# Softmax probabilities scaled on ScalarE instead of VectorE in a two-block transformer kernel

## The chip, the core and the metric

One core of a Trainium2 chip (trn2) runs the whole program in one launch. The metric is the device time of a launch in microseconds. The kernel before takes 810.37 us (median of three runs, 810.2 to 810.66).

## What is computed

256 tokens of width 1024 go through two transformer blocks. The first block is attention with 16 softmax heads of 64 columns and a feed-forward part with a short convolution. The second block is a feed-forward part, a mixer with 8 "stick-breaking" heads and 8 "forgetting" heads, and another feed-forward part. The change touches the 24 heads that end in a softmax: the 16 of the first block and the 8 forgetting ones. For these the reference computes:

```
p = softmax(where(k_pos <= q_pos, z, -inf), axis=-1)      # z = q k^T (+ forgetting terms)
out = einsum('bhqk,bhkd->bhqd', p, v)
```

The softmax divides each row of exponentials by the row's sum. With 256 queries and causal masking a head's exponentials take 128 x 384 numbers: 128 x 256 for the later 128 queries (all 256 keys) and 128 x 128 for the earlier ones.

## The kernel before, in words

The order of every instruction is fixed by one list of steps that a planner class writes before the program is built (`Plan.lay`). Each engine walks the same list and emits its own part of each step; an engine runs its instructions strictly in that order, and semaphores hold it where it needs another engine's result.

The bulk of the work is weight matmuls. A weight slab (8 tiles of 128 rows by 256 columns) is loaded by DMA into `raw`; ScalarE writes a rounded copy `whi` (L769) and VectorE the remainder `wlo` = raw - whi (L1015), both in pieces of two tiles (128 x 512); TensorE then does three matmuls per tile and half (hi x hi, hi x lo, lo x hi; L1442, L1445 and L1446, or L1431 to L1433 where the value columns are made). Twelve such matmuls make a chunk. After each chunk the planner puts one more `hi` step (and the `lo` step of the piece before it) and then lets the attention heads advance by one turn (`attend`), so attention is woven into the weight matmuls.

Heads go in pairs (n, n+1). Counted in turns from the pair's start (its age), the planner puts:

- age 0, `scores`: TensorE computes both heads' scores (L1496, for forgetting heads also L1504); VectorE adds the mask and takes the negated row maxima (L1333 and L1335, the two parts of a head, result in `rs`); ScalarE does the exponentials and row sums (L959 and L960).
- age 2, `scale` of head n: VectorE takes the reciprocals of the row sums (L1342) and multiplies the two parts of `W` by them (L1344: 128 x 256; L1345: 128 x 128), then raises `s_scale`.
- age 3, `turn` of head n, then `scale` of head n+1, then possibly `scores` of the next pair: TensorE transposes W in three pieces (L1513), which waits for `s_scale`; ScalarE copies the result out of PSUM (L967).
- age 4, `turn` of head n+1.
- age 6, `values`: TensorE multiplies by the values (L1550), ScalarE and VectorE split the result (L978 `Ohi`, L1365 `Olo`).

A second pair enters when the first has age 3, and the next two only when all is through, so the 24 softmax heads come in six sets of two pairs, four sets in the first block (about 22 us apart, from 26 us on) and two in the second (from 542 and from 593 us on). Each set has four turns of L1513; I call them turn 1 to turn 4 of the set.

Of the kernel before, what the change touches and what calls it, by code (L numbers as in the profile page):

```python
# [7 lines left out]
ALU = mybir.AluOpType  # L8
ACT = mybir.ActivationFunctionType
# [5 lines left out]
P = 128  # L15
S = 256
# [435 lines left out]
def build_program(nc, a, out):  # L452
    with ExitStack() as ctx:
        def sb(name, shape, dt=F32):
            return ctx.enter_context(nc.sbuf_tensor(name, shape, dt))

        def sem(name):
            return ctx.enter_context(nc.semaphore(name))
# [45 lines left out]
        rs = sb("rs", [P, 4, 4])  # L504
# [12 lines left out]
        W8 = sb("W8", [P, 8, 3 * P])  # L517
# [27 lines left out]
        s_scores, s_max, s_exp, s_inv, s_scale = (sem(n) for n in ("s_scores", "s_max", "s_exp", "s_inv", "s_scale"))  # L545
# [9 lines left out]
        soft = {n: k + 1 for k, n in enumerate(m for m, h in enumerate(heads) if h[0] != "sb")}  # L555
# [184 lines left out]
        def _(act):  # L740
            need = Once(act)
# [195 lines left out]
            def first_pass(n):  # L937
# [21 lines left out]
                act.activation(p[:, 0:S], b[:, 0:S], ACT.Exp, bias=m[:, 0:1], scale=-1.0, accum_out=s[:, 0:1])  # L959
                act.activation(p[:, S:3 * P], b[:, S:3 * P], ACT.Exp, bias=m[:, 1:2], scale=-1.0, accum_out=s[:, 1:2]).then_inc(s_exp, 1)  # L960

            def turned(n):
                i = n % 4
                need.wait_ge(s_tpe, t_use["turn", n] + 1)
                if n >= 4:
                    need.wait_ge(s_val, n // 2 - 1)
                act.activation(W8[:, 2 * i + 1, :], banks[T_BANK][:, 0:3 * P], ACT.Copy).then_inc(s_w, 1)  # L967
# [18 lines left out]
            def qk_norm(base):  # L986
# [8 lines left out]
                act.activation(lb, lb, ACT.Exp, scale=-0.5).then_inc(s_qr, 1)  # L995

            part_of = {"hi": weights, "ain": a_in, "gq": norm_columns, "sq": squares, "norm": norm, "latey": late_hi, "modul": shift_hi,
                       "ccol": condition, "evict": evict, "fpart": forget, "scores": first_passes, "turn": turned, "later": later,
                       "values": values, "vturn": v_turned, "qkn": qk_norm}
            for step in st.list:  # L1000
                if step[0] in part_of:
# [3 lines left out]
        def _(dve):  # L1005
            need = Once(dve)
# [268 lines left out]
            def values_out(g):  # L1275

                ph, _, c0 = groups[g]
                c = (qkv_base(ph, c0) - 16) * P
                if ph == "qkv1" and c == 0:
                    root_columns()  # L1280
                for i in range(2):
                    o = Vn[:, i, c:c + C]
                    if ph == "qkv1":
                        need.wait_ge(s_rcol, 2)
                        ins = dve.tensor_scalar(o, at(g, i), rcol[:, i:i + 1], None, ALU.mult)
                    else:
                        ins = dve.tensor_copy(o, at(g, i))
                ins.then_inc(s_evicted, 1)
# [47 lines left out]
                                         op0=ALU.add, op1=ALU.min, accum_out=m[:, 1:2]).then_inc(s_max, 1)  # L1336

            def scale(n):
                i = n % 4
                s, p = rs[:, i, 2:4], W8[:, 2 * i, :]  # L1340
                need.wait_ge(s_exp, soft[n])
                dve.reciprocal(s, s).then_inc(s_inv, 1)  # L1342
                need.wait_ge(s_inv, soft[n])
                dve.tensor_scalar(p[:, 0:S], p[:, 0:S], s[:, 0:1], None, ALU.mult)  # L1344
                dve.tensor_scalar(p[:, S:3 * P], p[:, S:3 * P], s[:, 1:2], None, ALU.mult).then_inc(s_scale, 1)  # L1345

            def stick_sum(n):
                i, k = n % 4, stick[n]
# [18 lines left out]
            def qk_norm(base):  # L1367
                need.wait_ge(s_qr, nth("qkn", base))
                need.wait_ge(s_gq, 1)
                for n in (base, base + 1):  # L1370
# [6 lines left out]
            part_of = {"lo": weights, "ain": a_in, "add": add_squares, "latey": late_y, "latelo": late_lo, "modul": modulate,  # L1377
                       "hcol": gates, "gq": first_columns, "mod": mod_dot, "modout": mod_out, "xscale": scale_x, "evict": evict, "fpart": forget,
                       "scores": peaks, "scale": scale, "stsum": stick_sum, "later": later, "values": values, "qkn": qk_norm}
            for step in st.list:  # L1380
                if step[0] in part_of:
# [231 lines left out]
```

## Time and profile before

| | us |
|---|---|
| median of three runs | 810.37 |
| the profiled execution, its own time | 810.29 |
| its span, from first to last instruction | 808.1 |
| TensorE matmul busy | 795.0 (98%) |
| VectorE busy | 649.5 (80%) |
| ScalarE busy | 483.2 (60%) |

The first row of the table is what is predicted. The profile is one execution; between its span and its own time lie 2.2 us. Matmuls overlap one another in the pipe, so "busy" of TensorE is the time in which at least one was under way. The granted TensorE clock is 1.00 in all but the last stretch. In the views, PE is TensorE's matmul side, PEld its weight loads, DVE is VectorE, ACT is ScalarE.

### The profile page before, as it was taken

How to read it: one execution, taken by the hardware profiler on the slowest of the kernel's cores; microseconds unless marked ns; L12 is line 12 of the kernel's file. 1: busy time of each engine (PE TensorE's matmuls, PEld its weight loads, DVE VectorE, ACT ScalarE, POOL GpSimd, SP SyncE). 2: the span in 40 equal slices, each digit the busy share in tenths (PEclk: the TensorE clock that was granted, in tenths of full speed). 3: DMA queues.
4: the chain of work that ended last, by engine and by line, in shares of the span. 5: the costliest groups of instructions: out<-in, count | busy, mean ns of one | idle time of the engine just before them, and what ended most of it. 6: DMA issues, size and time to landing. Idle time of an engine off the chain costs nothing.

```text
span 808.1 us, 16849 instructions
## 1 busy us (share of the span) xinstructions
PE 795.0 (98%) x6800; PEld 773.9 (96%) x6800; DVE 649.5 (80%) x1395; ACT 483.2 (60%) x1008; POOL 21.4 (3%) x53
## 2 busy tenths in 40 slices
PE   7999999999999999999999999899999999999998
PEld 7999999999999999999999999889789999999998
DVE  5899887988889897999988887977667996775551
ACT  6755566677666666745554646665656775555440
POOL 1000000000000000000000000700000000000000
PEclk9999999999999999999999999999999999999999
DMA  9777784656666987599999887545334578655540
GB/s 293 263 249 233 221 286 137 207 188 201 208 205 202 323 280 269 166 330 342 346 316 314 281 260 238 161 131 178 117 108 152 184 260 263 211 184 193 196 157 27
DMA packets 150014, 179.44 MB, mean 222 GB/s; under 512 B 5681, under 2 KB 139569, under 8 KB 149937
## 3 DMA queue, kind: packets, MB, share of 16 engines
q1 hardware_dynamic: 147680, 177.22, 66.7%
q8 instruction: 54, 0.88, 0.5%
q10 hardware_dynamic: 1232, 1.11, 0.4%
q0 software_dynamic: 1024, 0.03, 0.1%
q14 instruction: 24, 0.19, 0.1%
HBM read 177.27 MB, written 1.05 MB: 221 GB/s over the span
## 4 chain that ended last, share of the span: by engine, by line
PE 89%; DVE 5%; ACT 3%; DMA 1%; issue 1%; SPq 0%; DVEq 0%; ACTq 0%
PE bank L1442 26%; PE bank L1445 26%; PE bank L1446 26%; DVE wlo L1015 2%; PE bank L1431 2%; PE bank L1550 1%; PE bank L1433 1%; PE bank L1432 1%; DMA raw<-in_moba_w_qkv 1%; PE bank L1496 1%; PE bank L1513 1%; ACT whi L769 1%; PE bank L1534 1%; ACT W L959 0%; ACT W L960 0%
## 5 line engine op out<-in xcount | busy, mean ns | idle before, releaser
L1015 DVE TENSOR_TENSOR wlo<-raw,whi 128x512 fp32r<-128x512 f32 x528 | 342.3, 683 | 66.1 <-ACT whi L769 65.3
L769 ACT ACTIVATE whi<-raw 128x512 fp32r<-128x512 f32 x528 | 306.5, 622 | 95.8 <-PE bank L1446 86.5
L1442 PE MATMUL bank<-A,whi 128*128 128x256 f32 x1152 | 323.0, 280 | 3.4 <-DVE wlo L1015 2.4
L1445 PE MATMUL bank<-A,whi 128*128 128x256 f32 x1152 | 318.9, 277 | 0.1
L1446 PE MATMUL bank<-A,wlo 128*128 128x256 f32 x1152 | 318.5, 276 | 0.0
L1442 PEld LDWEIGHTS bank<-A,whi 128*128 128x128 f32 x1152 | 216.5, 188 | 5.6 <-DVE wlo L1015 3.0
L1445 PEld LDWEIGHTS bank<-A,whi 128*128 128x128 f32 x1152 | 216.4, 188 | 0.7 <-issue 0.5
L1446 PEld LDWEIGHTS bank<-A,wlo 128*128 128x128 f32 x1152 | 216.3, 188 | 0.0
L1442 PE MATMUL bank<-Hhi,whi 128*128 128x256 f32 x528 | 146.0, 276 | 0.0
L1446 PE MATMUL bank<-Hhi,wlo 128*128 128x256 f32 x528 | 145.7, 276 | 0.0
L1445 PE MATMUL bank<-Hlo,whi 128*128 128x256 f32 x528 | 145.7, 276 | 0.0
L1445 PEld LDWEIGHTS bank<-Hlo,whi 128*128 128x128 f32 x528 | 99.1, 188 | 0.0
L1442 PEld LDWEIGHTS bank<-Hhi,whi 128*128 128x128 f32 x528 | 99.1, 188 | 0.0
L1446 PEld LDWEIGHTS bank<-Hhi,wlo 128*128 128x128 f32 x528 | 99.1, 188 | 0.0
L1114 DVE SCALAR_TENSOR_TENSOR mring<-mring,cact 128x1024 f32<-128x1024 f32 x72 | 87.1, 1218 | 0.0
L1442 PE MATMUL bank<-B,whi 128*128 128x258 f32 (+1 forms) x184 | 52.8, 287 | 0.1
L926 ACT ACTIVATE Hhi<-hb 128x256 fp32r<-128x256 f32 x33 | 13.8, 418 | 64.3 <-DVE hb L1209 38.7
L1445 PE MATMUL bank<-B,whi 128*128 128x258 f32 (+1 forms) x184 | 52.3, 284 | 0.0
L1446 PE MATMUL bank<-B,wlo 128*128 128x258 f32 (+1 forms) x184 | 51.8, 282 | 0.0
L1175 DVE SCALAR_TENSOR_TENSOR ca<-bank,cols,ca 128x255 f32<-128x255 f32 (+1 forms) x88 | 36.4, 473 | 2.0 <-ACT ca L892 2.0
L1442 PE MATMUL bank<-Ohi,whi 128*128 128x256 f32 x128 | 36.8, 287 | 0.0
L1445 PE MATMUL bank<-Olo,whi 128*128 128x256 f32 x128 | 35.7, 279 | 0.0
(170 smaller groups left out, 960.8 us busy)
## 6 DMA issues: line engine op xcount, KB each, us to landing
mring<-in_w_mod SPq DMA_DIRECT2D x72, 512.0 KB, 6.1
raw<-in_ffn_w_up SPq DMA_DIRECT2D x22, 1024.0 KB, 5.1
raw<-in_w_gate SPq DMA_DIRECT2D x22, 1024.0 KB, 5.6
raw<-in_w_up SPq DMA_DIRECT2D x22, 1024.0 KB, 5.5
raw<-in_w_down SPq DMA_DIRECT2D x16, 1024.0 KB, 5.5
raw<-in_w_in SPq DMA_DIRECT2D x12, 1024.0 KB, 5.7
raw<-in_moba_w_qkv SPq DMA_DIRECT2D x11, 1024.0 KB, 5.3
raw<-in_ffn_w_down SPq DMA_DIRECT2D x8, 1024.0 KB, 5.3
```

The costliest lines, as they stand in the source:

```text
L769: act.activation(whi[:, i % SPL, k0:k1, 0:width], raw[:, i % RAW, k0:k1, 0:width], ACT.Copy).then_inc(s_whi, 1)
L926: act.activation(Hhi[:, n, :], hb[:, 0, :], ACT.Copy).then_inc(s_hhi, 1)
L1015: dve.tensor_tensor(lo, raw[:, i % RAW, k0:k1, 0:width], hi.bitcast(F32), ALU.subtract).then_inc(s_wlo, 1)
L1114: dve.scalar_tensor_tensor(out=w, in0=w, scalar=1.0, in1=cact[:, :], op0=ALU.mult, op1=ALU.mult, accum_out=msum[:, u:u + 1]).then_inc(s_ms ...
L1175: ins = dve.scalar_tensor_tensor(out=y[:, part:S], in0=at(g, i, 0, S - part), scalar=cvec[:, 2 - part, c:c + 1], in1=y[:, part:S], op0=ALU ...
L1431: pe.matmul(o, xh[:, q], hi, start=kg == 0 and not j, stop=False)
L1432: pe.matmul(o, xl[:, q], hi, start=False, stop=False)
L1433: ins = pe.matmul(o, xh[:, q], lo, start=False, stop=final and j == 1)
L1442: pe.matmul(o, hi, xh, start=kg == 0 and not (j and halved(g)), stop=False)
L1445: pe.matmul(o, hi, xl, start=False, stop=False)
L1446: ins = pe.matmul(o, lo, xh, start=False, stop=final and (j == 1 or not halved(g)))
L1496: ins = pe.matmul(b[:, o0:o1], q[:, q0:q0 + P], k[:, 0:o1 - o0], start=o0 == 0, stop=o0 > 0 and kind == "moba")
```

## The change

VectorE keeps the reciprocal. The two multiplications of each of the 24 softmax heads become two ScalarE instructions (function Copy with a per-partition scale read from `rs`), at the same step of the list. They wait for `s_inv`, the reciprocal's semaphore, and raise `s_scale` in VectorE's place. VectorE no longer waits for its own reciprocal.

```diff
--- before.py
+++ after.py
@@ -959,6 +959,13 @@
                 act.activation(p[:, 0:S], b[:, 0:S], ACT.Exp, bias=m[:, 0:1], scale=-1.0, accum_out=s[:, 0:1])
                 act.activation(p[:, S:3 * P], b[:, S:3 * P], ACT.Exp, bias=m[:, 1:2], scale=-1.0, accum_out=s[:, 1:2]).then_inc(s_exp, 1)
 
+            def scale(n):
+                i = n % 4
+                s, p = rs[:, i, 2:4], W8[:, 2 * i, :]
+                need.wait_ge(s_inv, soft[n])
+                act.activation(p[:, 0:S], p[:, 0:S], ACT.Copy, scale=s[:, 0:1])
+                act.activation(p[:, S:3 * P], p[:, S:3 * P], ACT.Copy, scale=s[:, 1:2]).then_inc(s_scale, 1)
+
             def turned(n):
                 i = n % 4
                 need.wait_ge(s_tpe, t_use["turn", n] + 1)
@@ -995,7 +1002,7 @@
                 act.activation(lb, lb, ACT.Exp, scale=-0.5).then_inc(s_qr, 1)
 
             part_of = {"hi": weights, "ain": a_in, "gq": norm_columns, "sq": squares, "norm": norm, "latey": late_hi, "modul": shift_hi,
-                       "ccol": condition, "evict": evict, "fpart": forget, "scores": first_passes, "turn": turned, "later": later,
+                       "ccol": condition, "evict": evict, "fpart": forget, "scores": first_passes, "scale": scale, "turn": turned, "later": later,
                        "values": values, "vturn": v_turned, "qkn": qk_norm}
             for step in st.list:
                 if step[0] in part_of:
@@ -1336,13 +1343,9 @@
                                          op0=ALU.add, op1=ALU.min, accum_out=m[:, 1:2]).then_inc(s_max, 1)
 
             def scale(n):
-                i = n % 4
-                s, p = rs[:, i, 2:4], W8[:, 2 * i, :]
+                s = rs[:, n % 4, 2:4]
                 need.wait_ge(s_exp, soft[n])
                 dve.reciprocal(s, s).then_inc(s_inv, 1)
-                need.wait_ge(s_inv, soft[n])
-                dve.tensor_scalar(p[:, 0:S], p[:, 0:S], s[:, 0:1], None, ALU.mult)
-                dve.tensor_scalar(p[:, S:3 * P], p[:, S:3 * P], s[:, 1:2], None, ALU.mult).then_inc(s_scale, 1)
 
             def stick_sum(n):
                 i, k = n % 4, stick[n]
```

Lines after the insertion move by 7 on the way down (ScalarE's copy of the transposed W, L967 before, is L974 after) and by 3 further on.

ScalarE's order in the first set, turns 1 and 2 (`W` the probabilities, `rs` the row sums or their inverses, `bank` a PSUM bank). Before:

```order
L769 ACTIVATE whi<-raw 128x512 [waits s_chunk]
L769 ACTIVATE whi<-raw 128x512 [waits s_chunk,s_raw1]
L769 ACTIVATE whi<-raw 128x512 [waits s_chunk]
L967 ACTIVATE W<-bank 128x384 [waits s_tpe]
L959 ACTIVATE W,rs<-bank,rs 128x256 [waits s_max]
L960 ACTIVATE W,rs<-bank,rs 128x128
```

ScalarE at the same place, after:

```order
L769 ACTIVATE whi<-raw 128x512 [waits s_chunk]
L769 ACTIVATE whi<-raw 128x512 [waits s_chunk,s_raw1]
L966 ACTIVATE W<-W,rs 128x256 [waits s_inv]
L967 ACTIVATE W<-W,rs 128x128
L769 ACTIVATE whi<-raw 128x512 [waits s_chunk]
L974 ACTIVATE W<-bank 128x384 [waits s_tpe]
L966 ACTIVATE W<-W,rs 128x256 [waits s_inv]
L967 ACTIVATE W<-W,rs 128x128
L959 ACTIVATE W,rs<-bank,rs 128x256 [waits s_max]
```

The scaling of head n now stands before the third weight conversion, and that of head n+1 behind the copy of head n's transposed W and ahead of the next pair's exponentials.

VectorE's order in the first set around turns 3 and 4. Before:

```order
L1015 TENSOR_TENSOR wlo<-raw,whi 128x512 [waits s_whi] x2
L1342 RECIPROCAL rs<-rs 128x2 [waits s_exp]
L1344 TENSOR_SCALAR W<-W,rs 128x256 [waits s_inv]
L1345 TENSOR_SCALAR W<-W,rs 128x128
L1143 SCALAR_TENSOR_TENSOR QKV<-bank,Rr 128x256 [waits s_chunk]
L1143 SCALAR_TENSOR_TENSOR QKV<-bank,Rr 128x256
L1015 TENSOR_TENSOR wlo<-raw,whi 128x512 [waits s_whi]
L1365 TENSOR_TENSOR Olo<-bank,Ohi 128x256 [waits s_ohi]
```

VectorE at the same place, after, up to the reciprocal of turn 4:

```order
L1022 TENSOR_TENSOR wlo<-raw,whi 128x512 [waits s_whi] x2
L1348 RECIPROCAL rs<-rs 128x2 [waits s_exp]
L1150 SCALAR_TENSOR_TENSOR QKV<-bank,Rr 128x256 [waits s_chunk]
L1150 SCALAR_TENSOR_TENSOR QKV<-bank,Rr 128x256
L1022 TENSOR_TENSOR wlo<-raw,whi 128x512 [waits s_whi]
L1368 TENSOR_TENSOR Olo<-bank,Ohi 128x256 [waits s_ohi]
L1348 RECIPROCAL rs<-rs 128x2 [waits s_exp]
```

The reciprocals keep their places between the same neighbours; only the multiplications behind them are gone.

ScalarE's order in the fourth set, turns 3 and 4. Before:

```order
L967 ACTIVATE W<-bank 128x384 [waits s_tpe]
L769 ACTIVATE whi<-raw 128x512 [waits s_chunk]
L769 ACTIVATE whi<-raw 128x512 [waits s_chunk,s_raw0]
L978 ACTIVATE Ohi<-bank 128x256 [waits s_val]
L967 ACTIVATE W<-bank 128x384 [waits s_tpe]
```

ScalarE at the same place, after:

```order
L974 ACTIVATE W<-bank 128x384 [waits s_tpe]
L769 ACTIVATE whi<-raw 128x512 [waits s_chunk]
L966 ACTIVATE W<-W,rs 128x256 [waits s_inv]
L967 ACTIVATE W<-W,rs 128x128
L769 ACTIVATE whi<-raw 128x512 [waits s_chunk,s_raw0]
L985 ACTIVATE Ohi<-bank 128x256 [waits s_val]
L974 ACTIVATE W<-bank 128x384 [waits s_tpe]
L966 ACTIVATE W<-W,rs 128x256 [waits s_inv]
L967 ACTIVATE W<-W,rs 128x128
```

Here the scaling of turn 3 stands between the two weight conversions, and `Ohi`, the split of the previous pair's output, comes behind both.

## Rows read from the trace of the kernel before

**Rows 1.** The page: busy time of each engine, share of the span, instructions.

```profile
PE 795.0 (98%) x6800; PEld 773.9 (96%) x6800; DVE 649.5 (80%) x1395; ACT 483.2 (60%) x1008; POOL 21.4 (3%) x53
```

**Rows 2.** Line L1513: releaser of TensorE's idle time, us in total, times.

```profile
  DVE W L1345: 3.0, 9
```

**Rows 3.** Timeline, second set, turns 1 and 2: start, us, engine, line, count, [idle, releaser].

```profile
52.32 1.68 ACT L769 ACTIVATE whi<-raw 128x512 fp32r<-128x512 f32 x3
52.99 0.69 DVE L1015 TENSOR_TENSOR wlo<-raw,whi 128x512 fp32r<-128x512 f32 x1 [0.35 <-ACT whi L769]
53.60 0.15 DVE L1342 RECIPROCAL rs<-rs 128x2 f32<-128x2 f32 x1
54.06 0.28 DVE L1345 TENSOR_SCALAR W<-W,rs 128x128 f32<-128x128 f32 x1
54.40 0.55 PE L1513 MATMUL bank<-identf,W 128*128 128x128 f32 x3
54.98 0.49 ACT L967 ACTIVATE W<-bank 128x384 f32<-128x384 f32 x1 [0.98 <-PE bank L1513]
56.43 0.14 DVE L1335 DVE_READ_ACCUMULATOR2_ANT rs<- 128x1 f32 x1
56.61 0.47 ACT L959 ACTIVATE W<-bank,rs 128x256 f32<-128x256 f32 x1 [1.13 <-DVE rs L1335]
57.22 0.49 PE L1513 MATMUL bank<-identf,W 128*128 128x128 f32 x3
58.20 0.69 DVE L1015 TENSOR_TENSOR wlo<-raw,whi 128x512 fp32r<-128x512 f32 x1
```

**Rows 4.** Timeline of TensorE: last matmuls before turn 1, first and second set.

```profile
31.48 0.28 PE L1446 MATMUL bank<-A,wlo 128*128 128x256 f32 x1
32.20 0.55 PE L1513 MATMUL bank<-identf,W 128*128 128x128 f32 x3 [0.45 <-DVE W L1345]
...
54.07 0.28 PE L1446 MATMUL bank<-A,wlo 128*128 128x256 f32 x1
```

**Rows 5.** ScalarE durations, ns min/median/max; then two L790 in a row in the timeline.

```profile
L790 ACT ACTIVATE B<-XT,gcol x24: 492/495/511, 265.8 to 625.5; 128x256 fp32r<-128x256 f32 x24
L959 ACT ACTIVATE W<-bank,rs x24: 472/475/476, 28.5 to 602.2; 128x256 f32<-128x256 f32 x24
L960 ACT ACTIVATE W<-bank,rs x24: 357/366/374, 29.0 to 602.6; 128x128 f32<-128x128 f32 x24
...
617.84 0.91 ACT L790 ACTIVATE B<-XT,gcol 128x256 fp32r<-128x256 f32 x2 [0.43 <-DVE XT L1260]
```

**Rows 6.** Timeline, second set, turns 3 and 4.

```profile
59.49 0.16 DVE L1342 RECIPROCAL rs<-rs 128x2 f32<-128x2 f32 x1
61.18 0.55 PE L1513 MATMUL bank<-identf,W 128*128 128x128 f32 x3
62.05 0.15 DVE L1342 RECIPROCAL rs<-rs 128x2 f32<-128x2 f32 x1
62.94 0.49 PE L1513 MATMUL bank<-identf,W 128*128 128x128 f32 x3
```

**Rows 7.** Timeline, fourth set, turns 3 and 4.

```profile
104.49 0.16 DVE L1342 RECIPROCAL rs<-rs 128x2 f32<-128x2 f32 x1
105.73 0.39 ACT L978 ACTIVATE Ohi<-bank 128x256 fp32r<-128x256 f32 x1 [0.54 <-PE bank L1550]
106.49 0.15 DVE L1342 RECIPROCAL rs<-rs 128x2 f32<-128x2 f32 x1
107.38 0.49 PE L1513 MATMUL bank<-identf,W 128*128 128x128 f32 x3
```

**Rows 8.** Timeline of TensorE between sets (35 matmuls) and before turn 1 (35 matmuls).

```profile
44.93 0.28 PE L1432 MATMUL bank<-whi,A 128*128 128x256 f32 x1
48.78 0.28 PE L1433 MATMUL bank<-wlo,A 128*128 128x256 f32 x1
50.07 0.28 PE L1432 MATMUL bank<-whi,A 128*128 128x256 f32 x1
```

## The prediction

> **What bounds the kernel now.** I read the busy times first: TensorE is busy 98% of the span, VectorE 80%, ScalarE 60% [rows 1]. So time on the other two engines costs something only where TensorE waits for it. Next I asked the view of line L1513, the transpose that takes the scaled probabilities, what its engine had waited for: the second multiplication, L1345, 3.0 us in 9 entries, both sides of TensorE together [rows 2]. That is the one place in which the edited lines hold the bounding engine. The timeline then shows which of the four turns of a set it is. In the second set the last weight matmul starts at 54.07; they start 0.12 apart, so turn 1 was due at 54.19, but starts at 54.40, 0.06 after L1345 ends (54.06 + 0.28 = 54.34) [rows 3, 4]. In the first set it was due at 31.60 and starts at 32.20 [rows 4]. All six sets have turn 1 tied to L1345 in this way. The other turns follow the matmul ahead of them at the usual distance: they don't wait.
>
> **What is removed.** Per head VectorE loses two multiplications; from the end of the reciprocal (53.60 + 0.15 = 53.75) to the end of the second they take 0.59 us [rows 3]. The reciprocal itself keeps its place. What stands in front of it is L1015, which had VectorE idle for 0.35 waiting for ScalarE's `whi`, not for VectorE's own work [rows 3]; so freeing VectorE doesn't bring the reciprocal forward, and its saved time (24 heads) is worth nothing to turn 1. It makes later `wlo` pieces earlier, for which TensorE isn't waiting.
>
> **What is added.** The trace has no Copy of 128 x 256 or 128 x 128 within `W` with a pointer scale. The nearest row is L790, the same function with a pointer scale from SBUF to SBUF, 128 x 256: 0.495 us; two in a row take 0.91, so the second starts 0.41 after the first [rows 5]. The 128 x 128 part: 0.495 less the difference between the exponentials of the two sizes (0.475 - 0.366 = 0.11), so 0.385 [rows 5]. The pair: 0.41 + 0.385 = 0.80. The hand-over from VectorE to ScalarE costs 0.04 (56.43 + 0.14 = 56.57 to 56.61 [rows 3]). From the end of the reciprocal to ready probabilities: 0.84 in place of 0.59.
>
> As bounds of the pair: 0.5, if the two overlapped wholly (then turn 1 would gain 0.05), and 0.99, if the short one cost as much as the long one and nothing overlapped. I take 0.80, since L790 is the same instruction in all but its output tile. The Trainium skill (ScalarE: Activation LUTs, What ACT_TABLE_LOAD costs) gives 186 ns + 0.833 ns per element, 93 ns more for each pointer operand and 93 ns overlap between neighbours; worked out from it, an estimate, the pair is 0.40 + 0.39 = 0.79. By that rule the sum below would be 0.1 us less; the trace agrees on the long part (0.492 by the rule, 0.495 measured [rows 5]).
>
> **Turn 1, six sets.** ScalarE is free in time: of the three `whi` pieces from 52.32 on [rows 3], two stand ahead of the scaling now and leave the queue at 53.36. Scaling starts at 53.79, ends at 54.59, and TensorE starts 0.06 later: 0.25 later than now. Since it waits already, all of it is on the path: 6 x 0.25 = **1.50 us**.
>
> **Turn 2.** The scaling of head n+1 now stands behind ScalarE's copy of turn 1 (54.98 + 0.49, and 0.25 later: 55.72) and ends by 56.52; turn 2 is due at 57.22 + 0.25 = 57.47 [rows 3]. Hidden. What is queued behind it on ScalarE are the next pair's exponentials at 56.61 + 0.25 = 56.86, which wait for the row maxima, and these for TensorE; hidden as well, by 0.3.
>
> **Turn 3.** The reciprocal ends at 59.65, the scaling at 60.49, turn 3 is due at 61.18 [rows 6]. Hidden.
>
> **Turn 4.** The reciprocal ends at 62.20, the scaling at 63.04, TensorE could start at 63.10, and turn 4 is due at 62.94 [rows 6]: a new wait of 0.16. Five sets have this spacing to within 0.02: 5 x 0.16 = **0.80 us**. In the fourth set a second `whi` piece stands between the scaling of turn 3 and `Ohi`. The reciprocal ends at 104.65, so the scaling runs from 104.69 and leaves the queue 0.70 later (0.80 less the 0.10 by which neighbours overlap); that piece takes 0.52 and `Ohi` starts at 105.92 instead of 105.73. `Olo` and the reciprocal at 106.49 come 0.19 later, and turn 4 starts at 106.83 + 0.84 + 0.06 = 107.73 instead of 107.38 [rows 7]: **0.35 us**.
>
> **Restart.** A turn that had to wait takes 0.55 for its three transposes, one that didn't 0.49 (54.40 and 57.22 [rows 3]), since its weight load had not run ahead. Six turns 4 go from one kind to the other: 6 x 0.06 = **0.36 us**.
>
> **Weights.** The third `whi` piece comes about 1.1 us later (behind the scaling: to 55.1 instead of 54.0), but VectorE turns to that piece's `wlo` only at 58.20 [rows 3]. Hidden.
>
> **Sum.** 1.50 + 0.80 + 0.35 + 0.36 = 3.0 us on the profiled execution's 810.29 us (the 2.2 us outside its span stay). The median is 0.08 higher. I predict **813.3 us**. With the pair at 0.5 the same sum gives 810.0; with 0.99, each of the twelve waits 0.19 longer, 815.6. Its own range, for what I believe of the pair and the hand-overs (0.75 to 0.85): 812.4 to 814.2.
>
> **Rivals.**
>
> *Within the noise.* A measurement of this kernel can tell some 0.2% (1.6 us) from no change. If the scaling overlaps better than L790 does (pair 0.65), turn 1 costs 0.10, turn 4 waits nowhere but in the fourth set (0.20, and 0.06): 810.29 + 0.9 = 811.2. For it: neither instruction converts its output, as L790's does. Against: L790, in 24 instances, never takes less than 0.492 [rows 5].
>
> *All 24 turns pay.* The Trainium skill (ScalarE: Activation LUTs, Rules for kernel authors) sends multiplications to VectorE rather than ScalarE; here the rows give 0.84 for 0.59. If ScalarE, in order, ran so late that each head's 0.25 reached TensorE: 24 x 0.25 = 6.0, so 816.3. For it: ScalarE's added work sits in short bursts. Against: turns 2 and 3 have 0.9 and 0.6 in hand in the second set.
>
> *The matmul cadence changes.* Before turn 1 TensorE starts matmuls (54.07 - 50.07) / 34 = 117.6 ns apart, between sets (48.78 - 44.93) / 34 = 113.2 ns [rows 4, 8]; the wait at turn 1 seems to end the slower pace, and I don't know why. If the new wait at turn 4 set off the slower one for the 60 matmuls up to the next scores: 60 x 4.4 ns x 6 = 1.6 more, 814.9. If instead it ended a slow stretch behind the last set of each block (some 100 matmuls each): 0.9 less, 812.4.
>
> *Faster.* The place is turn 1, the mechanism the freed VectorE: if `wlo` ahead of the reciprocal was held by VectorE's own backlog, the reciprocal would come earlier, and from 0.25 earlier on turn 1 would gain. At most the present waits go: 0.60 + 5 x 0.21 = 1.65; so 808.6. For it: VectorE is busy 80% overall. Against: the 0.35 of idle time ahead of that very `wlo` [rows 3].
>
> **How the numbers follow.** Forecast 0.60; within the noise 0.13; all 24 turns 0.07; slower cadence 0.08; faster cadence 0.08; faster kernel 0.04. Slower by over 0.2%: 0.60 + 0.07 + 0.08 + 0.08 = 0.83; within 0.2% 0.13; faster 0.04. The range 811.4 to 814.9 holds the forecast's own, both cadences and a tip of the noise case.
>
> **What would show it.** Right: L966 at 0.49 and L967 at 0.39 us, TensorE's wait before turn 1 longer by 0.25 in six sets, a wait of 0.16 before turn 4 (0.35 in the fourth set), none at turns 2 and 3, VectorE idle more, the reciprocal at its old distance from the scores. Wrong: L966 shorter than 0.45, a reciprocal that comes earlier, a wait for `wlo` inside the sets, or a span that grew by more than the waits at L1513.

## The result, and the profile after

| | before | after |
|---|---|---|
| median, us (six runs each) | 810.51 (810.07 to 812.5) | 813.25 (813.01 to 814.23) |
| the profiled execution, its own time | 810.29 | 813.83 |
| its span | 808.1 | 811.6 |

The changed kernel is slower: 1.0036 times the time before, 95% interval 1.0026 to 1.0046, so 2.1 to 3.7 us more. Forecast were 813.3 us. Two single executions among those of the experiments, 2042 us of the kernel before and 2809 us of the run with fixed scales, are slow ones, and the ratios and intervals leave them out.

The page of the changed kernel answers [rows 1]:

```profile
PE 797.9 (98%) x6800; PEld 775.7 (96%) x6800; DVE 636.7 (78%) x1347; ACT 501.3 (62%) x1056; POOL 21.3 (3%) x53
```

VectorE lost 12.8 us of busy time and ScalarE gained 18.1, both off the bounding engine for the most part. What reached TensorE is in the views of the two new lines and of the transposes (L1516 now):

```profile
L966 ACT ACTIVATE W<-W,rs x24: 498/509/513, 31.2 to 610.4; 128x256 f32<-128x256 f32 x24
  DVE rs L1348: 1.9, 6
L967 ACT ACTIVATE W<-W,rs x24: 385/387/392, 31.6 to 610.8; 128x128 f32<-128x128 f32 x24
  PEld bank L1516: 5.2, 13
  PE bank L1516: 2.7, 7
```

```profile
  ACT W L967: 7.9, 20
```

Where TensorE's two sides waited 3.0 us for VectorE in 9 entries [rows 2], they now wait 7.9 for ScalarE in 20 (the last row, of L1516). ScalarE itself sat waiting for a reciprocal only 6 times, one per set: that is turn 1. In the other 18 heads no idle time of ScalarE is put down to it.

The timeline of the second set at turns 1 and 2, in answer to [rows 3, 4] (start, us, engine, line, count, idle before):

```profile
52.55 1.16 ACT L769 ACTIVATE whi<-raw 128x512 fp32r<-128x512 f32 x2
53.22 0.69 DVE L1022 TENSOR_TENSOR wlo<-raw,whi 128x512 fp32r<-128x512 f32 x1 [0.35 <-ACT whi L769]
53.83 0.15 DVE L1348 RECIPROCAL rs<-rs 128x2 f32<-128x2 f32 x1
54.02 0.51 ACT L966 ACTIVATE W<-W,rs 128x256 f32<-128x256 f32 x1 [0.31 <-DVE rs L1348]
54.21 0.28 PE L1449 MATMUL bank<-A,wlo 128*128 128x256 f32 x1
54.44 0.39 ACT L967 ACTIVATE W<-W,rs 128x128 f32<-128x128 f32 x1
54.88 0.55 PE L1516 MATMUL bank<-identf,W 128*128 128x128 f32 x3 [0.39 <-ACT W L967]
56.24 0.39 ACT L967 ACTIVATE W<-W,rs 128x128 f32<-128x128 f32 x1
57.60 0.29 PE L1449 MATMUL bank<-A,wlo 128*128 128x256 f32 x1
57.73 0.49 PE L1516 MATMUL bank<-identf,W 128*128 128x128 f32 x3
```

The `wlo` ahead of the reciprocal still waits 0.35 for `whi`, as before. From the end of the reciprocal (53.98) to the end of the scaling (54.83) it is 0.85 where VectorE needed 0.59. Turn 1 starts at 54.88, 0.05 behind the end of the scaling and 0.67 behind the start of the last matmul, where it was 0.33. (That distance also depends on how fast the 36 matmuls ahead of it ran. The distance from the scores, used below, doesn't: it is 0.25 longer.) Turn 2 starts 0.13 behind its last matmul, its scaling having ended at 56.63.

Turns 3 and 4 of the same set, in answer to [rows 6]:

```profile
61.69 0.55 PE L1516 MATMUL bank<-identf,W 128*128 128x128 f32 x3
62.56 0.16 DVE L1348 RECIPROCAL rs<-rs 128x2 f32<-128x2 f32 x1
62.75 0.51 ACT L966 ACTIVATE W<-W,rs 128x256 f32<-128x256 f32 x1
63.17 0.39 ACT L967 ACTIVATE W<-W,rs 128x128 f32<-128x128 f32 x1
63.61 0.55 PE L1516 MATMUL bank<-identf,W 128*128 128x128 f32 x3
```

Turn 4 starts 1.92 after turn 3, where it was 1.76 [rows 6], and it is now directly behind the scaling (63.56). Its three transposes take 0.55 instead of 0.49. In the fourth set, in answer to [rows 7]:

```profile
106.96 0.61 ACT L769 ACTIVATE whi<-raw 128x512 fp32r<-128x512 f32 x1
107.19 0.55 PE L1516 MATMUL bank<-identf,W 128*128 128x128 f32 x3
107.48 0.36 ACT L985 ACTIVATE Ohi<-bank 128x256 fp32r<-128x256 f32 x1
108.22 0.15 DVE L1348 RECIPROCAL rs<-rs 128x2 f32<-128x2 f32 x1
108.82 0.39 ACT L967 ACTIVATE W<-W,rs 128x128 f32<-128x128 f32 x1
109.26 0.55 PE L1516 MATMUL bank<-identf,W 128*128 128x128 f32 x3 [0.16 <-ACT W L967]
```

Here `Ohi` starts directly behind the delayed `whi` piece, and turn 4 is 2.07 behind turn 3. Before it was 1.77, with turn 3 at 105.61.

I measured every set against its own scores and its own neighbours, which leaves the pace of the weight matmuls out:

| us | sets 1 to 6, before | after | difference |
|---|---|---|---|
| scores to turn 1 | 5.80, 5.41, 5.41, 5.41, 5.79, 5.79 | 6.05, 5.67, 5.66, 5.67, 6.04, 6.04 | 4 x 0.25 + 2 x 0.26 = 1.52 |
| last matmul to turn 4 | 0.12 in all | 0.27, 0.28, 0.27, 0.43, 0.28, 0.27 | 3 x 0.15 + 2 x 0.16 + 0.31 = 1.08 |
| the transposes of turn 4 | 0.49 | 0.55 | 6 x 0.06 = 0.36 |

Together 2.96 us from rows that are rounded to 0.01; in the nanoseconds of the trace the three are 1.48, 1.09 and 0.33, together 2.90. The medians differ by 2.74, the two profiled spans by 3.5. The surplus of the latter is taken apart below, with the repetition of the changed kernel.

### The profile page after: what moved, and what is told of

It is laid out like the page before. It is cut to its first block, busy times and chain, and to the rows that moved or that the text cites. A ratio compares the mean times of both kernels' runs of the same rounds, so it can differ in the third digit from the quotient of the medians.

```text
span 811.6 us, 16849 instructions
## 1 busy us (share of the span) xinstructions
PE 797.9 (98%) x6800; PEld 775.7 (96%) x6800; DVE 636.7 (78%) x1347; ACT 501.3 (62%) x1056; POOL 21.3 (3%) x53
## 3 DMA queue, kind: packets, MB, share of 16 engines
HBM read 177.27 MB, written 1.05 MB: 220 GB/s over the span
## 4 chain that ended last, share of the span: by engine, by line
PE 87%; DVE 5%; ACT 4%; issue 1%; DMA 1%; SPq 0%; DVEq 0%; ACTq 0%
PE bank L1445 26%; PE bank L1448 26%; PE bank L1449 25%; DVE wlo L1022 2%; PE bank L1434 2%; PE bank L1553 1%; PE bank L1436 1%; PE bank L1435 1%; DMA raw<-in_moba_w_qkv 1%; PE bank L1516 1%; PE bank L1499 1%; ACT whi L769 1%; ACT W L960 1%; ACT W L959 1%; PE bank L1537 1%
```

## The experiments

Theory A is that of the prediction: a head costs something only where TensorE is behind the scaling already (turn 1) or comes within its reach (turn 4), and then by the difference in duration. The rivals stand in the expectations as they were written. In the diffs `<` is the kernel that the experiment starts from, `>` the experiment, a line with neither is only there for orientation, and `...` marks what is left out; comments in them are mine.

**Only the turn-1 heads on ScalarE.** From the changed kernel; the scaling stays on ScalarE for one head in four, the first of each set, and goes back to VectorE for the other three.

```diff
> ON_ACT = (0,)
...
  def scale(n):                         # ScalarE
>     if n % 4 not in ON_ACT:
>         return
...
  def scale(n):                         # VectorE, behind the reciprocal
...
>     if n % 4 in ON_ACT:
>         return
>     p = W8[:, 2 * (n % 4), :]
>     need.wait_ge(s_inv, soft[n])
>     need.wait_ge(s_scale, soft[n] - 1)
...                                     # the two multiplications as in the kernel before
```

> ScalarE scales only the heads of turn 1 (first head of each set of four); VectorE scales the other three as before. Theory A (a delay of the probabilities reaches TensorE one to one where TensorE waits for them, and nowhere else): turn 1 starts 0.25 us later after its scores in each of six sets, no new wait before turn 4, so +1.5 us, 812.0. Rival B (each head moved to ScalarE costs the same, through ScalarE's occupancy): a quarter of the changed kernel's +2.7 us, so +0.7, 811.2. Either may be off by up to 1 us through the matmul pace, 113.5 or 117.8 ns, in stretches that the change doesn't touch; the waits in the profile tell A from B.

Measured: 811.9 us (811.43 to 812.54), before on the same chip 810.4; ratio 1.0017, 1.0007 to 1.0027. Turn 1 is 0.58 or 0.59 behind the last matmul in the second to fourth sets, where it was 0.33 before, and turn 4 is 0.12 behind it in all six sets. Turn 1 of the second set:

```profile
54.44 0.55 PE L1526 MATMUL bank<-identf,W 128*128 128x128 f32 x3 [0.31 <-ACT W L970]
```

The 1.5 us are the six turns 1, and the waits at turn 4 need the fourth head on ScalarE. The time alone would not have said so: the 811.2 of rival B lies inside the interval too. The timeline and the next run rule it out.

**Only the heads of turns 2 and 3 on ScalarE.** From the run above. Twelve heads, twice as many as there.

```diff
< ON_ACT = (0,)
> ON_ACT = (1, 2)
```

> ScalarE scales only the heads of turns 2 and 3; VectorE those of turns 1 and 4, as before. Theory A: both are hidden, turn 1 keeps its old wait; in the fourth set alone the scaling ahead of Ohi moves the reciprocal by 0.19 us, so turn 4 there waits some 0.1 us and restarts 0.06 dearer: +0.15 us, 810.7. Rival B: half of the +2.7, so +1.4, 811.9.

Measured: 810.33 us (810.09 to 810.77), before 810.4; ratio 0.9999, 0.9989 to 1.0009. Twelve heads moved and the time did not, within its interval of 0.1%. What ended the idle time before the transposes (L1526 of this kernel) was VectorE's multiplication in 8 entries and ScalarE's scaling in one (the 5 called "issue" are no wait for another engine):

```profile
  DVE W L1358: 2.5, 8
  issue: 0.9, 5
  ACT W L970: 0.2, 1
```

One small wait did appear, 0.10 before turn 4 of the fourth set: the `whi` piece, `Ohi` and the reciprocal come later there by the scaling of turn 3, as the prediction had it, only without the last 0.25. A cost that goes by the number of heads is excluded by this pair of runs: six heads cost 1.5 us, twelve others none.

**The same two instructions, each shorter.** From the changed kernel; both take a fixed scale in place of the pointer, so the probabilities are not normalised.

```diff
< act.activation(p[:, 0:S], p[:, 0:S], ACT.Copy, scale=s[:, 0:1])
< act.activation(p[:, S:3 * P], p[:, S:3 * P], ACT.Copy, scale=s[:, 1:2])...
> act.activation(p[:, 0:S], p[:, 0:S], ACT.Copy, scale=0.01)
> act.activation(p[:, S:3 * P], p[:, S:3 * P], ACT.Copy, scale=0.01)...
```

> The changed kernel with the fixed scale 0.01 in place of the pointer to the inverse row sum: the probabilities are not normalized. All waits and the order stay. Theory A (the length of the two ScalarE instructions is the price): each instruction is some 0.09 us shorter, the pair 0.61 to 0.62 instead of 0.80, so turn 1 comes 0.06 us later than in the kernel before, turn 4 doesn't wait in any set: +0.4 us on 810.5, 810.9. Rival C (the place in ScalarE's queue and the hand-over are the price): as the changed kernel, 813.2.

Measured: 810.66 us, before 810.4; ratio 1.0003, 0.9994 to 1.0013. Timeline of the second set, turn 1:

```profile
53.15 0.16 DVE L1348 RECIPROCAL rs<-rs 128x2 f32<-128x2 f32 x1
53.34 0.42 ACT L966 ACTIVATE W<-W 128x256 f32<-128x256 f32 x1 [0.32 <-DVE rs L1348]
53.67 0.29 ACT L967 ACTIVATE W<-W 128x128 f32<-128x128 f32 x1
54.01 0.55 PE L1516 MATMUL bank<-identf,W 128*128 128x128 f32 x3
```

Without its pointer each instruction is shorter by 0.09 us (medians 0.509 and 0.418, 0.387 and 0.294). From the end of the reciprocal (53.31) to the end of the scaling (53.96) it is 0.65, or 0.06 more than on VectorE, and counted from the scores turn 1 is 0.07 later than before in the second to fourth sets. Turn 4 starts without a wait in all six sets, though its three transposes take 0.52 instead of 0.49. With the same instructions in the same places, 2.5 of the 2.7 us are gone. So it is the duration, not the place in ScalarE's queue or the change of engine as such. The Trainium skill (ScalarE: Activation LUTs, What ACT_TABLE_LOAD costs) puts 93 ns on each pointer operand; this pair of kernels agrees, with 0.51 against 0.42 and 0.39 against 0.29.

**Three instructions instead of two.** From the changed kernel, the 128 x 256 part in two halves.

```diff
< act.activation(p[:, 0:S], p[:, 0:S], ACT.Copy, scale=s[:, 0:1])
> act.activation(p[:, 0:P], p[:, 0:P], ACT.Copy, scale=s[:, 0:1])
> act.activation(p[:, P:S], p[:, P:S], ACT.Copy, scale=s[:, 0:1])
```

> The changed kernel with the 128 x 256 part scaled in two instructions of 128 x 128: three instead of two per head, same result. Theory A: the first part takes 0.30 + 0.30 instead of 0.41 us, so the probabilities are ready 0.19 us later; turn 1 and turn 4 wait 0.19 longer each in six sets (12 x 0.19 = 2.3), the fourth set's turn 4 another 0.19: +2.5 us on the changed kernel, 815.7. Rival B (24 heads alike): 24 x 0.19 = 4.6, 817.8. Rival C (place in the queue, not length): 813.2.

Measured: 815.4 us (815.19 to 815.64), before 810.4; ratio 1.0063, 1.0047 to 1.0079. The second set's turn 1:

```profile
54.43 0.40 ACT L966 ACTIVATE W<-W,rs 128x128 f32<-128x128 f32 x1 [0.31 <-DVE rs L1349]
54.74 0.39 ACT L967 ACTIVATE W<-W,rs 128x128 f32<-128x128 f32 x1
55.03 0.39 ACT L968 ACTIVATE W<-W,rs 128x128 f32<-128x128 f32 x1
55.47 0.55 PE L1517 MATMUL bank<-identf,W 128*128 128x128 f32 x3 [0.49 <-ACT W L968]
```

The scaling takes 0.99 instead of 0.81, and turn 4 is 0.46 behind its last matmul instead of 0.27 in five sets, 0.69 instead of 0.43 in the fourth, where turn 3 waits too (0.11). Twelve times some 0.19 is 2.3 us; the difference to before grew from 2.7 to 5.0. The cost goes up with the duration at the same twelve places, as it went down in the run before; the 817.8 of rival B (24 heads alike) lies outside the interval.

**Turn 1's scaling earlier, on VectorE.** From the kernel before. If turn 1 waits for the reciprocal, and that for the `wlo` ahead of it, which waits for `whi`, then putting the reciprocal and the multiplications ahead of that `wlo` should take turn 1's wait away altogether.

```diff
< for step in st.list:                  # VectorE's walk of the list
> order = list(st.list)
> for n in range(0, len(heads), 4):
>     if n in soft:
>         k = order.index(("scale", n))
>         j = max(m for m in range(k) if order[m][0] == "lo")
>         order.insert(j, order.pop(k))
> for step in order:
```

> The kernel before (all scaling on VectorE), but in VectorE's order the reciprocal and multiplications of turn 1's head stand ahead of the wlo piece instead of behind it. Theory A: the probabilities of turn 1 are ready 0.6 us or more before TensorE is due, all its waits there go: 0.60 in the first set, 0.21 in sets 2 to 4, 0.35 in sets 5 and 6, and six restarts of 0.06: 2.3 us less, 808.1. Rival D (the wait at turn 1 is what ends the slow matmul pace of 117.8 ns, which then lasts through the set): up to 150 more matmuls per set at 4.3 ns more, 6 x 0.65 = 3.9 us dearer, so 812. In between, by how far the slow pace reaches.

Measured: 808.62 us (807.96 to 809.77), before 810.3; ratio 0.9978, 0.9969 to 0.9987: faster than both kernels. Timeline of the second set:

```profile
51.48 1.68 ACT L769 ACTIVATE whi<-raw 128x512 fp32r<-128x512 f32 x3
51.72 0.15 DVE L1342 RECIPROCAL rs<-rs 128x2 f32<-128x2 f32 x1
52.18 0.28 DVE L1345 TENSOR_SCALAR W<-W,rs 128x128 f32<-128x128 f32 x1
52.38 1.28 DVE L1015 TENSOR_TENSOR wlo<-raw,whi 128x512 fp32r<-128x512 f32 x2
53.22 0.28 PE L1452 MATMUL bank<-A,wlo 128*128 128x256 f32 x1
53.34 0.49 PE L1519 MATMUL bank<-identf,W 128*128 128x128 f32 x3
```

The probabilities are ready at 52.46 and turn 1 starts at 53.34, 0.12 behind the last matmul; so in all six sets. Scores to turn 1 shrank by 0.60, 3 x 0.21 and 2 x 0.35, which is 1.93 us, and the transposes of turn 1 take 0.49 again, another 0.33. The medians show 1.7 us of these 2.3; the last section takes the profile apart.

**Turn 1's reciprocal earlier, scaling on ScalarE.** The same edit of VectorE's walk on the changed kernel, so that ScalarE's scaling never waits for the reciprocal.

```diff
> order.insert(j, order.pop(k))         # as above, VectorE only
```

> The changed kernel (scaling on ScalarE) with the reciprocal of turn 1's head ahead of the wlo piece in VectorE's order. ScalarE then starts the scaling as soon as its two whi pieces are through (53.36 in the second set's old times, not 53.79). Theory A: turn 1 comes 0.42 us earlier than in the changed kernel in six sets, turn 4 waits as there: 2.5 us less than 813.25, 810.7. Rival C (the reciprocal is not what turn 1 waits for on ScalarE): 813.2.

Measured: 810.4 us (810.01 to 811.59), before 810.3; ratio 0.9999, 0.9989 to 1.0008. The second set:

```profile
52.30 1.16 ACT L769 ACTIVATE whi<-raw 128x512 fp32r<-128x512 f32 x2
52.54 0.15 DVE L1348 RECIPROCAL rs<-rs 128x2 f32<-128x2 f32 x1
53.34 0.51 ACT L966 ACTIVATE W<-W,rs 128x256 f32<-128x256 f32 x1
53.74 0.40 ACT L967 ACTIVATE W<-W,rs 128x128 f32<-128x128 f32 x1
54.19 0.55 PE L1522 MATMUL bank<-identf,W 128*128 128x128 f32 x3
```

The reciprocal is there at 52.69, but ScalarE comes to the scaling only behind its two `whi` pieces, at 53.34, and turn 1 misses its due time by 0.03. Turn 4 keeps its wait (0.27, 0.43 in the fourth set), since nothing was moved there. With the reciprocal out of the way the change costs 1.8 us (810.4 against the 808.62 of the run before). Between the two profiles the sets show more than that. Turn 4 has 1.09 and its restarts 0.33. Counted from the scores, turn 1 is later by 0.41 in the first set, 0.03 in the second to fourth and 0.17 in the last two, which is 0.84, and its restarts cost 0.33 again. That is 2.6. Against it the run before lost some 1.2 to slower matmuls in its profile, as the last section tells, which leaves 1.4; the medians' 1.8 lies between.

**A one-column matmul behind the scores.** From the run with early multiplications on VectorE. There TensorE's weight matmuls kept a slow pace, 117.8 ns from start to start, in stretches that ran at 113.4 to 114.0 ns before (last section). The kernel before has matmuls of one column (L1426) behind which the pace was fast; this puts one behind the first scores of each of the first block's sets.

```diff
> if kind == "moba" and n % 4 == 0:     # "moba": the heads of the first block
>     t_free("turn", n)
>     pe.matmul(banks[T_BANK][:, 511:512], meanf[:, :], meanf[:, 0:1], start=True, stop=True)
```

> The kernel of e5_early_vector with one more matmul, of one column, behind the scores of the first pair in the four sets of the first block (its result is not used). Theory A with a pace that such a matmul sets back: TensorE starts the 36 matmuls before turn 1 at 113.5 instead of 117.8 ns, 4 x 0.16 = 0.6 us less than e5, less 4 x 0.03 for the matmul itself, 807.6; if e5 is slow by rival D, this one regains up to 2.6 us of it. If the extra matmul doesn't set the pace, the same as e5.

Measured: 808.92 us (808.59 to 809.95), before 810.3; ratio 0.9983, 0.9974 to 0.9991. No gain over 808.62, against the 807.6 expected. The 36 matmuls before turn 1 do run at 115.1 ns instead of 117.6, but with the one-column matmul in front of them scores to turn 1 takes 5.33 us instead of 5.20, and the twelve behind the second scores go from 113.3 ns up to 117.7 in three of the four sets (in the first they were slow already). The 24 behind turn 2, in turn, run at 113.5 or 113.6 ns in all four, where they ran at 117.8. The idea of a free reset falls.

**The changed kernel again, and the kernel before again.** No edit; one profile each.

> The changed kernel once more, for its profile. In its first profile 240 matmuls behind the first norm (134.9 to 163.2 us) ran 117.8 ns apart, in the kernel before 113.3, which is 1.06 us of the difference of the two spans. If that pace belongs to the execution, not to the kernel, this profile can have it at 113.3 and a span of 810.5 us; the waits before turns 1 and 4 must be the same to 0.02 us either way. If it belongs to the changed kernel, 117.8 again.

> The kernel before once more, for its profile. If the pace behind the first norm belongs to the execution, it is 113.3 or 117.8 ns, with a span of 808 or 809 us; distances from scores to turn 1 of 5.41 us (first block, sets 2 to 4) and 5.79 us (second block), as in its first profile.

> The changed kernel, unaltered, executed a third time, to see whether the pace of its 240 matmuls behind the first norm (117.8 ns per matmul in its two profiles so far, 113.3 in both of the kernel before) belongs to the kernel or to the execution. If it belongs to the kernel: 117.8 again, and a profiled execution of 813 to 814 us. If it belongs to the execution: 113.3 can appear, and then the profiled execution lies about 1.06 us lower, near 812.8. In both cases the distances before the transposes of turn 1 and turn 4 stay as they were (turn 1 0.25 us above those of the kernel before, turn 4 0.27 us behind the last matmul).

Measured: 815.81, 810.09 and 812.80 us, and the 240 matmuls behind the first norm at 117.8, 113.3 and 113.3 ns. The 815.81 holds one stretch in which the granted clock fell. Two rows of the windows view of that profile (us, busy and instructions of PE, PEld, DVE, ACT and POOL, granted clock, DMA share, GB/s):

```profile
520.00:525.00 5.00, 3.38 (x17) 3.13 (x16) 4.86 (x12) 4.87 (x11) 5.00 (x12) 0.70 0.74 214
525.00:530.00 5.00, 5.00 (x40) 4.44 (x39) 3.85 (x8) 1.82 (x4) 2.65 (x6) 0.96 0.97 301
```

Means of 0.70 and 0.96 over 5 us each are 3.4 us at the lower level, 1.2 GHz. Of the 2.0 us by which this profile is behind the first one, 0.3 are there at the scores ahead of that stretch (519 us) and all 2.0 at the next ones (529 us): the fall of the clock cost 1.7. The third profile has 1.00 and 39 matmuls in the same window. In both TensorE had just stood idle for 1.6 us (until 521.87 and 520.55, for VectorE's L1168), and in the other ten profiles for 1.5 to 1.6 at the same place, with the clock at 1.00 throughout. So an idle time of that length is followed by the lower level in one execution and not in another. It does not lie at the changed heads.

In the third profile the first norm's stretch is back at the pace of the kernel before. The timeline of TensorE, the first matmul behind the norm and the last of the 240; first of the changed kernel's first profile, then of its third:

```profile
134.93 0.36 PE L1445 MATMUL bank<-A,whi 128*128 128x256 f32 x1
...
163.16 0.28 PE L1449 MATMUL bank<-A,wlo 128*128 128x256 f32 x1
```

```profile
135.09 0.36 PE L1445 MATMUL bank<-A,whi 128*128 128x256 f32 x1
...
162.26 0.28 PE L1449 MATMUL bank<-A,wlo 128*128 128x256 f32 x1
```

That is 28.23 against 27.17 us for the same work of the same program: 1.06 us that the change does not need. The slow 28.23 also came up in the kernel with early multiplications on VectorE, in which ScalarE scales nothing, and in the one with the early reciprocal and ScalarE's scaling; the other eight of the twelve profiles have the fast 27.17 or 27.18. Whether the change makes the slow one more frequent can't be told from so few.

With this the 3.5 us between the two first profiles can be taken apart: 2.90 in the sets, 1.05 behind the first norm, 2 x 0.15 from 36 matmuls at the slow pace behind the first and third sets, less 0.38 by which the first set's scores started earlier (26.01 instead of 26.40) and 0.39 in the stretch between the fourth set and the norm. The last two also differ between the two profiles of the kernel before, by 0.34 and 0.42. The third profile, whose first scores start at 26.38, is 2.5 us over the kernel before (810.6 against 808.1). Of what the sets took in the first profile the third shows 0.25 less, in one place: the first set's reciprocal ends 0.25 sooner behind the scores (4.76 to its start instead of 5.00), so turn 1 is where it was before. The first set of one and the same program swings by this much.

## Why the prediction was right, point by point

- *Durations.* Forecast were 0.495 and 0.385 for the two instructions, 0.80 for the pair and 0.84 with the hand-over. Measured: 0.509, 0.387, 0.81 (54.02 to 54.83) and 0.85. L790 was the right row to read, 0.014 short for the long part.
- *Turn 1, 1.50 us.* Measured 1.52 (1.48 in nanoseconds), about 0.25 in each set, and the run with only these heads costs 1.5.
- *Freed VectorE.* The idle 0.35 ahead of the `wlo` was the right thing to ask for: with both multiplications gone it is still 0.35, the reciprocal keeps its distance from the scores, and the rival *Faster* falls. The early-multiplication run shows the other half: the reciprocal's place in the order is what counts. The price of that rival was worked out wrongly, though: it took 0.21 for each of five sets, but the fifth and sixth wait 0.35, and it left out the restarts. The waits to be gained were 1.95 us with 0.33 behind them, 2.3 instead of 1.65. That the early multiplications came to 808.62, next to its 808.6, is a coincidence: they gained more at turn 1 and lost part of it to the pace.
- *Turns 2 and 3, hidden.* The run with twelve of these heads on ScalarE costs nothing. *All 24 turns pay* falls.
- *Turn 4, 0.80 + 0.35.* Measured 0.77 and 0.31. The mechanism of the fourth set was right in each step (the second `whi` piece behind the scaling of turn 3, `Ohi`, `Olo`, the reciprocal); it came out 0.04 shorter: counted from turn 3, `Ohi` came 0.17 later instead of 0.19, and it took 0.36 instead of 0.39.
- *Restart, 0.36 us.* Six turns 4 at 0.55 instead of 0.49 (0.33 in nanoseconds): as forecast. But the rule was put too narrowly. Turn 3 takes 0.55 in every set of both kernels [rows 6] though it waits for no scaling; its weight load does not run ahead of the matmuls either (61.17 against 61.18 in the kernel before, 62.85 against 62.94 at turn 4). With fixed scales the load of turn 4 leads by 0.04 and they take 0.52. So the 0.55 goes with the weight load, not with the wait.
- *Within the noise.* It needed a pair of 0.65. The instruction pair measured 0.81; the run with fixed scales (0.62 from 53.34 to 53.96) shows what would have followed, no difference.
- *The matmul cadence changes.* The pace does change, and in the changed kernel's first profile in both directions that I gave: the 36 matmuls between turn 4 and the next scores are slow after two of three sets (0.15 us each), and the stretch behind the fourth set is 0.39 faster. But neither needs the wait at turn 4. The changed kernel's third profile has neither. The kernel before, in its second profile, has the slow matmuls too, behind its second set, and the fast stretch behind the fourth. I was right to hold a chance for it and wrong in its cause.

The mechanism and its terms are confirmed one by one. That 813.3 met the median of 813.25 to 0.05 us is luck all the same: the difference came out at 2.74 where I had 2.93 over a base of 810.37, and the base was 0.14 higher with more executions (810.51). The pace of the matmuls alone moves one execution by 1 us.

What stays open is the last 0.2 us: 2.90 in the sets against 2.74 between the medians. The swing of the first set (0.25) is of that size.

## What to carry to other kernels

On a kernel whose bounding engine is busy 98% of the time, an edit of the other engines is worth, to first order, what it adds or takes at the few places where the bounding engine waits or nearly does: find those places, take the slack of each from the timeline, and set the added duration against it. Here 0.26 us more per head cost 2.7 us at 12 of 24 places and nothing at the other 12. The remedy for the wait at turn 1 was here neither a faster instruction nor another engine but an earlier place in the queue: the reciprocal and its multiplications stood behind a piece that was itself waiting, and moving them ahead of it gave 1.7 us.

## What the runs showed of the hardware that was not expected

The same matmuls (128 x 128 weights, 256 columns) run at two paces, some 113.4 and 117.8 ns from start to start, with the granted clock at 1.00 in both and no engine waiting. One program shows both in the same place (the 240 matmuls above). What sets either pace, I did not find.

The waits at turn 1 go with the fast pace, but are not shown to be its cause. With a wait at turn 1 the 24 matmuls behind turn 2 run at 113.5 to 114.0 ns in 27 of the 30 sets of the five profiles of the two kernels. Where the early multiplications took that wait away, they run at 117.8 in all six sets. Against a simple rule stands the run with the one-column matmul: no wait at turn 1 either, and the same 24 run at 113.5 in the four sets of the first block. Nor does a one-column matmul reliably end the slow pace: in the changed kernel's first profile the 240 slow matmuls follow directly on two of them (L1429).

With the early multiplications the slow pace also went on to the next set. TensorE's timeline of that kernel, in answer to the first two of [rows 8]:

```profile
44.17 0.28 PE L1437 MATMUL bank<-whi,A 128*128 128x256 f32 x1
...
47.94 0.28 PE L1439 MATMUL bank<-wlo,A 128*128 128x256 f32 x1
```

From 44.17 to 47.94 are 32 intervals of 117.8 ns; in the kernel before it was 113.2 between sets. The 36 matmuls take 4.23 us instead of 4.07, the 24 ahead of them 2.79 instead of 2.71, and this in three places.

The span of this profile, 807.1, is 1.0 us under that of the kernel before, and it comes out as follows. Turn 1 gave back 1.95 us and its restarts 0.33. The slow pace in and between the sets took 1.2 of that again, 0.75 of it in the three places above. Besides, the 240 matmuls behind the first norm were slow (1.06 dearer), while the first set's scores started 0.55 earlier and the stretch between the fourth set and the norm took 0.40 less; these three differ between executions of one kernel as well. The profile's own time, 809.42, is 0.8 above the median of 808.62, so the 1.7 us between the medians can't be shared out from it. What it does show is that taking a wait away was worth less than its length, since slower matmuls took part of it.
